# The expert loop of a hybrid decoder layer: down halves moved into the next pass, weight chunks of 1024 columns, SwiGLU on halves

## The reference, cut to what matters

```python
def moe(x2d, w_router, b_router, w_in, b_in, w_out, b_out):
    logits = (x2d @ w_router).astype(jnp.float32) + b_router.astype(jnp.float32)
    top_val, top_idx = lax.top_k(logits, TOP_K)
    gates = jax.nn.softmax(top_val, axis=-1)
    ...
    def expert_block(args):
        xb, e = args
        h = xb @ w_in[e] + b_in[e]
        glu = jnp.minimum(h[:, ::2], SWIGLU_LIMIT)
        lin = jnp.clip(h[:, 1::2], -SWIGLU_LIMIT, SWIGLU_LIMIT)
        act = glu * jax.nn.sigmoid(SWIGLU_ALPHA * glu) * (lin + 1.0)
        return act @ w_out[e] + b_out[e]
    ...
    y = y_buf[dest] * g_s[:, None].astype(y_buf.dtype)
    return jax.ops.segment_sum(y, tok_s, num_segments=N)
```

## Time and profile before

| what | value |
|---|---|
| median of 3 runs | 1720.86 us (1720.2 to 1728.64) |
| the profiled execution | 1725.17 us, of which the span of the trace is 1723.1 us |
| TensorE matmul busy | 1598.6 us (93%), 7671 instructions |
| TensorE weight load busy | 1259.6 us (73%) |
| VectorE busy | 1446.1 us (84%) |
| ScalarE busy | 1027.0 us (60%) |
| GpSimd busy | 153.7 us (9%) |
| DMA in a stretch of six passes | 95% of the 16 engines' time, 339 GB/s |
| mean granted TensorE clock | 0.956 of full |

### The profile page before, as it was taken

The page is one execution under the profiler, slowest core; times in us unless marked ns, Lnnn a source line. Parts: engine busy times, 40 slices in busy tenths (PEclk is TensorE's granted clock), DMA queues, the critical chain, the costliest instruction groups (busy, mean ns, idle before and its releaser), DMA issues.

```text
span 1723.1 us, 25611 instructions
## 1 busy us (share of the span) xinstructions
PE 1598.6 (93%) x7671; PEld 1259.6 (73%) x7671; DVE 1446.1 (84%) x1996; ACT 1027.0 (60%) x1067; POOL 153.7 (9%) x102
## 2 busy tenths in 40 slices
PE   3999688969999999999999999999999999999991
PEld 3999466737777777777777777777777777777771
DVE  4542742368999999999999999999999999999997
ACT  4221531226667666666776666676677666667673
POOL 0000311000010001000001000010000110001000
PEclk9999778959999999999999999999999999999996
DMA  7200701017999999999999999999999999999976
GB/s 249 98 26 1 245 0 43 25 37 272 344 331 351 339 338 338 346 341 336 346 333 347 343 337 349 336 343 334 335 350 334 340 347 341 336 344 347 337 271 249
DMA packets 243213, 476.46 MB, mean 277 GB/s; under 512 B 12784, under 2 KB 29808, under 8 KB 243120
## 3 DMA queue, kind: packets, MB, share of 16 engines
q1 hardware_dynamic: 229472, 445.23, 73.6%
q0 software_dynamic: 10128, 28.06, 4.4%
q10 hardware_dynamic: 3584, 2.78, 0.5%
HBM read 463.45 MB, written 21.50 MB: 281 GB/s over the span
## 4 chain that ended last, share of the span: by engine, by line
DVE 48%; issue 21%; ACT 3%; DVEq 3%; DMA 1%; SPq 0%
DVE split L1386 31%; DVE work L1402 3%; DVE work L1406 3%; ACT work L998 3%; DVE work L1399 3%; DVE operands L1392 1%; DVE work L1360 1%; DVE operands L1413 1%; DVEq L1347 1%; DMA ring<-expert_rows 1%; DVE operands L1381 1%; DVEq L124 0%; DVEq L1385 0%; DVE ring L1484 0%; DVE gate_next L1371 0%
## 5 line engine op out<-in xcount | busy, mean ns | idle before, releaser
L1386 DVE TENSOR_TENSOR split<-ring,split 128x2048 fp32r<-128x2048 f32 x398 | 892.5, 2283 | 4.0
L988 ACT CAST split<-ring 128x2048 fp32r<-128x2048 f32 x399 | 762.5, 1914 | 120.1 <-PE pair L789 113.0
L785 PE MATMUL pair<-split,operands 128*128 128x512 f32 x1584 | 650.4, 411 | 4.4 <-issue 4.4
L786 PE MATMUL pair<-split,operands 128*128 128x512 f32 x1584 | 628.4, 397 | 0.0
L789 PE MATMUL pair<-split,operands 128*128 128x512 f32 x1584 | 438.9, 399 | 7.9 <-DVE split L1386 7.9
L785 PEld LDWEIGHTS pair<-split,operands 128*128 128x128 f32 x1584 | 298.8, 189 | 98.0 <-issue 36.8
L789 PEld LDWEIGHTS pair<-split,operands 128*128 128x128 f32 x1584 | 293.4, 189 | 95.7 <-DVE split L1386 28.0
L786 PEld LDWEIGHTS pair<-split,operands 128*128 128x128 f32 x1584 | 298.8, 189 | 61.9
L998 ACT ACTIVATE work<-work 128x256 f32<-128x256 f32 x132 | 55.2, 418 | 251.8 <-DVE work L1399 251.8
L1546 POOL DMA_INDIRECT expert_rows<-work,dest_cur x33 | 84.0, 2545 | 665.8 <-ACT work L1011 625.2
L544 PE MATMUL pair<-split,operands 128*128 128x256 f32 x384 | 94.6, 284 | 8.6 <-issue 8.6
(11 more groups left out here) (205 smaller groups left out, 1299.3 us busy)
## 6 DMA issues: line engine op xcount, KB each, us to landing
ring<-in_w_moe_in SPq DMA_DIRECT2D x264, 1024.0 KB, 6.8
ring<-in_w_moe_out SPq DMA_DIRECT2D x132, 1024.0 KB, 6.8
ring<-in_w_in SPq DMA_DIRECT2D x12, 1024.0 KB, 10.9
ring<-expert_rows SPq DMA_DIRECT2D x3, 2048.0 KB, 10.1
late_ring<-in_w_o SPq DMA_DIRECT2D x4, 1024.0 KB, 9.6
resid<-in_x SPq DMA_DIRECT2D x4, 512.0 KB, 6.8
h_rows<-work ACTq DMA_DIRECT2D x4, 512.0 KB, 2.7
late_ring<-expert_rows SPq DMA_DIRECT2D x4, 512.0 KB, 9.0
```

Source lines behind the costliest of these rows:

```text
L785: pe.matmul(dst, left_hi[:, k0 + k, :], hi[s][:, k, :], start=(start and k == 0), stop=False)
L786: pe.matmul(dst, left_lo[:, k0 + k, :], hi[s][:, k, :], start=False, stop=False)
L988: act.copy(hi[j % PARTS], raw[j % RAW]).then_inc(hi_made, 1)
L1386: dve.tensor_tensor(lo[j % PARTS], raw[j % RAW], hi[j % PARTS].bitcast(F32), ALU.subtract).then_inc(lo_made, 1)
```

## The change

- **Order of the work.** The down products of pass p - 1 are moved into pass p, between the two halves of its up products. A pass is now: 4 chunks of the first up half of its expert, 4 down chunks of the expert before, 4 chunks of the second up half. The first pass has only the 8 up chunks, and four down chunks follow the last pass. The dummy chunks after the last pass are gone, and `parts` use the ring's slots in another order with other waits.
- **Chunks.** A chunk is now 256 rows of 1024 columns (still 1 MB; each row of it is 4 KB in a piece, where it was 2 KB). A product still has 12 matmuls of 512 columns, now two rows' blocks by two banks.
- **Bias.** `pick_bias` and `b_in_parts` span 128 partitions, the added ones zero, and the bias of a half is two matmuls of 128 rows. GpSimd adds 1 to the odd biases once.
- **SwiGLU.** Two halves of 512 results each: the sigmoid reads PSUM directly, and VectorE has three operations of 512 columns.
- **Token list.** `onehot` and `route_cur` are float32r, so that the list is four matmuls of that type; the gate's rest is the fourth column. VectorE builds the one-hot in one operation.
- **GpSimd.** It takes over `prepare_list` (three copies and a subtraction), `pick` (one copy) and the copies of destination and gate (`keep_lists`, three), eight small operations a pass which read SBUF. The scatter of pass p - 1 stands in pass p.
- **Transposes.** The activations' are two groups of four; the token rows' eight are two groups of four in different places, ahead of the last two up products.

```diff
-GW = 512
 KH = KT // 2
+HALF = 1024
+QUARTERS = KT // 2
 CHUNKS = 12
-IN_CHUNKS = 8
+DOWN, SECOND = 4, 8
 RAW = 6
 PARTS = 3
 SLOTS = P
 MAX_PASSES = SEQ * TOPK // SLOTS + NE - 1
-AHEAD = 3
-LO_AHEAD = 2
-STEPS_PER_PASS = 13
+STEPS_PER_PASS = 4
+STEPS_TO_ROUTE = 5
+ACT_LIMIT = LIMIT / (1.0 + math.exp(-SWI_ALPHA * LIMIT))
...
+raw = [ring[:, s].rearrange("p k c -> p (k c)").rearrange("p (k c) -> p k c", c=HALF) for s in range(RAW)]
...
+def up_chunk(e, half, k):
+    rows = of_expert(w_moe_in, e).rearrange("e (a k p) c -> a (e p) k c", p=P, a=QUARTERS)[k]
+    return rows[:, :, half * HALF:(half + 1) * HALF]
+def down_chunk(e, k):
+    return of_expert(w_moe_out, e).rearrange("e (a k p) c -> a (e p) k c", p=P, a=QUARTERS)[k]
+class Step:
+    def __init__(self, p, j):
+        first = isinstance(p, int) and p == 0 and j < DOWN
+        self.number = j if first else p * CHUNKS + (j - DOWN)
+        self.slot = j if first else (j + 2) % RAW
+        self.buffer = j % PARTS if first else (j + 2) % PARTS
+        self.fill = 1 if first else p * 2 + (j + 2) // RAW
...
+    def load(p, j, src):
+        c = Step(p, j)
+        sp.wait_ge(hi_made, c.number + (1 - RAW))
+        sp.wait_ge(lo_made, c.number + (1 - RAW))
+        sp.dma_start(raw[c.slot], src).then_inc(raw_full[c.slot], 16)
...
     def one_pass(p):
+        e, before = expert_of(p), expert_of(p - 1)
+        for k in range(QUARTERS):
+            load(p, k, up_chunk(e, 0, k))
+        for k in range(QUARTERS):
+            load(p, DOWN + k, down_chunk(before, k))
+        for k in range(QUARTERS):
+            load(p, SECOND + k, up_chunk(e, 1, k))
...
+    done = after_last(sp)
+    last = expert_of(done - 1)
+    for k in range(QUARTERS):
+        load(done, k, down_chunk(last, k))
...
+            sp.wait_ge(hi_made, all_used + (-4, -2, 0)[r])
+            sp.wait_ge(lo_made, all_used + (-4, -2, 0)[r])
...
     def product(p, j, dst, k0, left_hi, left_lo, start, stop):
+        pe.wait_ge(hi_made, c.number + 1)
+        for k in range(2):
+            for f in range(2):
+                cols = slice(f * 512, (f + 1) * 512)
+                pe.matmul(dst[:, f, :], left_hi[:, k0 + k, :], hi[c.buffer][:, k, cols],
+                          start=(start and k == 0), stop=False)
+                pe.matmul(dst[:, f, :], left_lo[:, k0 + k, :], hi[c.buffer][:, k, cols],
+                          start=False, stop=False)
+        pe.wait_ge(lo_made, c.number + 1)
+        for k in range(2):
+            for f in range(2):
+                cols = slice(f * 512, (f + 1) * 512)
+                mm = pe.matmul(dst[:, f, :], left_hi[:, k0 + k, :], lo[c.buffer][:, k, cols],
+                               start=False, stop=(stop and k == 1))
...
+    def bias_of_half(g):
+        for f in range(2):
+            at_f = (2 * g + f) * 512
+            pe.matmul(pair[g][:, f, :], pick_bias, b_in_parts[:, at_f:at_f + 512], start=True, stop=False)
+    def up(p, g, k):
+        product(p, g * SECOND + k, pair[g], 2 * k, xT_hi, xT_lo, False, k == QUARTERS - 1)
+    def down(p, j, k):
+        product(p, j, pair[2], 2 * k, actT_hi, actT_lo, k == 0, k == QUARTERS - 1)
...
+    def first_half(p, before):
+        pe.wait_ge(pick_ready, p + 1)
+        if before:
+            pe.wait_ge(half_read, p * 2 - 1)
+        bias_of_half(0)
+        pe.wait_ge(xT_lo_made, p * 2 + 1)
+        up(p, 0, 0)
+        up(p, 0, 1)
+        pe.wait_ge(xT_lo_made, p * 2 + 2)
+        up(p, 0, 2)
+        if before:
+            act_transposes(p - 1, 1)
+        up(p, 0, 3)
+    def second_half(p, before):
+        if before:
+            pe.wait_ge(half_read, p * 2)
+        bias_of_half(1)
+        up(p, 1, 0)
+        act_transposes(p, 0)
+        up(p, 1, 1)
+        pe.wait_ge(idx_ready, p + 2)
+        x_transposes(p + 1, 0)
+        up(p, 1, 2)
+        pe.wait_ge(actT_lo_made, p * 2 + 1)
+        x_transposes(p + 1, 1)
+        up(p, 1, 3)
...
     def one_pass(p):
+        first_half(p, True)
+        pe.wait_ge(down_banks_free, p)
+        pe.wait_ge(actT_lo_made, p * 2 - 1)
+        down(p, DOWN, 0)
+        token_list(p + 1)
+        down(p, DOWN + 1, 1)
+        pe.wait_ge(actT_lo_made, p * 2)
+        down(p, DOWN + 2, 2)
+        down(p, DOWN + 3, 3)
+        second_half(p, True)
...
+    done = after_last(pe)
+    pe.wait_ge(down_banks_free, done)
+    down(done, 0, 0)
+    act_transposes(done - 1, 1)
+    down(done, 1, 1)
+    pe.wait_ge(actT_lo_made, done * 2)
+    down(done, 2, 2)
+    down(done, 3, 3)
...
     def sigmoid(p, g):
+        last = Step(p, g * SECOND + QUARTERS - 1)
+        act.wait_ge(chunk_used, last.number + 1)
+        if not (isinstance(p, int) and p == 0 and g == 0):
+            act.wait_ge(act_ready, p * 2 + g)
+        glu = pair[g].rearrange("p b (c a) -> p a b c", a=2)[:, 0]
+        act.activation(sig.rearrange("p (b c) -> p b c", b=2), glu, ACT.Sigmoid, scale=SWI_ALPHA)\
+            .then_inc(sig_ready, 1)
...
+    def scale_rows(p, j):
+        act.wait_ge(chunk_used, Step(p, j).number + 1)
+        act.wait_ge(lists_kept, p + 1)
+        act.activation(y_rows.rearrange("p (f c) -> p f c", f=2), pair[2][:, :, :], ACT.Copy, scale=gate_cur[:, 0:1])\
+            .then_inc(down_banks_free, 1)
...
     def one_pass(p):
+        x_hi(p, 0)
+        make_hi(p, 0)
+        make_hi(p, 1)
+        x_hi(p, 1)
+        make_hi(p, 2)
+        sigmoid(p - 1, 1)
+        make_hi(p, 3)
+        make_hi(p, 4)
+        make_hi(p, 5)
+        act_hi(p - 1, 1)
+        make_hi(p, 6)
+        sigmoid(p, 0)
+        for j in range(7, 11):
+            make_hi(p, j)
+        scale_rows(p, DOWN + 3)
+        act_hi(p, 0)
+        make_hi(p, 11)
...
+    def slots_one_hot(p):
+        dve.wait_ge(route_ready, p + 1)
+        dve.tensor_tensor(onehot, slot_id.unsqueeze(1).to_broadcast([P, NT, SLOTS]),
+                          slot_from[:, :].unsqueeze(2).to_broadcast([P, NT, SLOTS]), ALU.is_equal)\
+            .then_inc(onehot_ready, 1)
...
+        wait(dve, lists_kept, p)
+        chain(dve.tensor_scalar(list_next[:, 0:1], bank[6][:, 0:1], NOWHERE, None, ALU.add))
+        chain(dve.tensor_reduce(list_next[:, 1:2], bank[6][:, 2:4], AX_X, ALU.add))
+        chain.settle()
+        dve.tensor_copy(token_next[:, :], bank[6][:, 1:2]).then_inc(idx_ready, 1)
...
     def swiglu(p, g):
+        glu, shifted = (pair[g].rearrange("p b (c a) -> p a b c", a=2)[:, a] for a in range(2))
+        gate, line, result = (m.rearrange("p (b c) -> p b c", b=2) for m in (sig, lin, act_rows[:, g, :]))
+        dve.wait_ge(sig_ready, p * 2 + (g + 1))
+        chain(dve.tensor_scalar(line, shifted, LIMIT + 1.0, 1.0 - LIMIT, ALU.min, ALU.max))
+        dve.scalar_tensor_tensor(gate, glu, LIMIT, gate, ALU.min, ALU.mult).then_inc(half_read, 1)
+        chain.settle()
+        dve.wait_ge(half_read, p * 2 + (g + 1))
+        dve.scalar_tensor_tensor(result, gate, ACT_LIMIT, line, ALU.min, ALU.mult).then_inc(act_ready, 1)
...
     def one_pass(p):
+        x_lo(p, 0)
+        make_lo(p, 0)
+        make_lo(p, 1)
+        x_lo(p, 1)
+        make_lo(p, 2)
+        swiglu(p - 1, 1)
+        make_lo(p, 3)
+        make_lo(p, 4)
+        slots_one_hot(p + 1)
+        make_lo(p, 5)
+        act_lo(p - 1, 1)
+        make_lo(p, 6)
+        swiglu(p, 0)
+        make_lo(p, 7)
+        read_list(p + 1)
+        for j in range(8, 11):
+            make_lo(p, j)
+        act_lo(p, 0)
+        make_lo(p, 11)
...
+    for still in (b_in_parts[2 * NE:P, :], pick_bias[2 * NE:P, :]):
+        dve.memset(still.bitcast(F32), 0.0).then_inc(b_in_split, 1)
...
+    def prepare_list(p, e):
+        if not (isinstance(p, int) and p == 0):
+            pool.wait_ge(list_ready, p)
+            pool.sem_inc(pool_passed, 1)
+        chain(pool.tensor_copy(first_cur[:, :], col(pass_first, p)))
+        chain(pool.tensor_copy(route_cur.unsqueeze(2), of(route, e)))
+        chain(pool.tensor_copy(pos_cur[:, :].unsqueeze(2), of(slot_of, e)))
+        chain.settle()
+        pool.sem_inc(pool_passed, 1)
+        pool.tensor_scalar(slot_from[:, :], pos_cur[:, :], first_cur[:, 0:1], None, ALU.subtract)\
+            .then_inc(route_ready, 1)
+    def pick(p, e):
+        if not (isinstance(p, int) and p == 0):
+            pool.wait_ge(chunk_used, Step(p - 1, SECOND).number + 1)
+            pool.sem_inc(pool_passed, 1)
+        pool.tensor_copy(pick_bias[0:2 * NE, :], col(expert_rows, e).to_broadcast([2 * NE, SLOTS]))\
+            .then_inc(pick_ready, 1)
...
+    def keep_lists(cur):
+        if cur:
+            chain(pool.tensor_copy(dest_cur[:, :], list_mid[:, 0:1]))
+            chain(pool.tensor_copy(gate_cur[:, :], list_mid[:, 1:2]))
+            chain.settle()
+            pool.sem_inc(pool_passed, 1)
+        pool.tensor_copy(list_mid[:, :], list_next[:, :]).then_inc(lists_kept, 1)
...
     def one_pass(p):
+        following = expert_of(p + 1)
+        prepare_list(p + 1, following)
         gather(p + 1)
-        scatter(p)
```

(61 more changed lines are left out.)

348 lines of the change are left out of this document (119 added, 229 removed).

## The result

The changed kernel takes 1740.96 us (median of 4 runs, 1739.97 to 1747.88) against 1723.76 us for the kernel before beside it: ratio 1.0106, 95% interval 1.0083 to 1.0129. It is 1% slower; 1640 us was predicted. The profiled execution took 1740.34 us, its span is 1738.5 us. One execution of a later kernel (the one whose sums wait, 1640.85 us) took 3866.52 us; it is left out of every ratio, and no run tells its cause.

What follows compares the result with a forecast made beforehand. VectorE was taken as full at 39.1 us a pass, TensorE hardly less. From 1723.1 us, 33 passes at 37.0 us give -73, start -3.7, pass 0 +3.8, end -8: 1642 us span, 1640 us median, range 1622 to 1705.

Steps and rivals of the forecast that it cites:

- TensorE's pass, 37.0 us: Loop pass on TensorE: products 33.7, bias 0.9, token list 0.45, transposes 1.9 us; 37.0 us for 39.24 before.
- the low end that was chosen: Bias on TensorE: 0.23 us per matmul of 128 rows, range 0.23 to 0.52; the high end costs 1.2 us a pass.
- VectorE's pass, 33.8 us: Loop pass on VectorE: its operations sum to 33.8 us, 5.3 us less than now, so VectorE stops being the bound.
- The gather: Next pass's token rows: landing at 28.2 us, wanted by TensorE at 30.0 us; 1.8 us of slack, the smallest found.
- The gather is late: Rival, chance 0.17: lo operations hold the gather; a second one makes TensorE wait 1.5 us in 32 passes, 1688 us.
- DMA doesn't set the pace: Rival, chance 0.08: if DMA's mean can't pass 350 GB/s, a pass takes 38.0 us, 1672 us in all.
- GpSimd's small operations: Rival, chance 0.10: lo holds the operations before the token list, the list is 4 to 5 us late, about 1800 us.
- Start: Kernel start: with the first x_lo ahead, the first product starts at about 386.9 us, worth -3.7 us.
- Pass 0's wait: First pass, without down products: its gather takes 10.3 us against 6.5 us of TensorE's work, +3.8 us.
- End: After the last product: without dummies the first three parts are summed earlier, sums near 1702, worth -8 us.
- The sum: Whole kernel: 1723.1 - 73 - 3.7 + 3.8 - 8 = 1642 us of span, 1640 us for the median.

## Why the prediction was wrong, point by point

- **TensorE's pass, 37.0 us:** right. At full clock it is busy 36.96 us; two bias matmuls take 1089.41 - 1088.95 = 0.46 us, the low end that was chosen. Without waits a pass takes 36.76 us.
- **VectorE's pass, 33.8 us:** 34.2 us, right.
- **The gather, "the rows land 6.3 us on the earlier trace rows, at 28.2 ... 1.8 us of slack":** this is the step that failed. The dates were right (start at 21.86 us, wanted at 29.95 us); the landing, taken from a gather among short operations, was 3.6 us too short. It comes at 31.8 us, 1.8 us late, and each us of wait costs a third more by the clock. The text had this outcome as a rival, *The gather is late*, and gave it 0.17 and 1688 us. Its evidence, a scatter of 2.60 us under lo, already spoke for a hold in the order that was forecast, and the forecast's own slack was smaller than one lo. But the rival had the way to it half wrong. It took one lo to hold the gather for 1.3 us and the rows to be still in time then, at 29.3 (28.2 + 1.3 is 29.5), and needed a second lo for its 31.5. The trace shows one lo, 1.1 us, and 2.5 us more between the instruction's end and the landing, for which the rival had no price, only "more if 4 KB packets of weights crowd it"; 2 KB packets gave 0.7 us of it. Its 1.5 us a pass were too small as well, for 1.95 of wait and, for the clock, nothing where 0.63 us a pass on average were lost (37.58 - 36.95).
- **The other rivals.** DMA doesn't set the pace of after: the kernels with the gather in time move 363 to 365 GB/s for 1,000 us. Their DMA share is 0.98 to 0.99, though, so little is left there. GpSimd's small operations are held, up to 2.32 us, 35 of the loop's 248 for over 2 us, but 0.6 us on average, and slot_from is ready at 1091.1, 9 us before VectorE's one-hot at 1100.18: not starved. The Trainium skill ("SBUF — State Buffer", section "Who interferes with whom") has such operations exclude each other, and the trace agrees: the copy that starts at 1088.17 under a lo lasts 2.04 us, to 1090.21. The same section reports that a tensor_tensor of VectorE, as lo is, was not seen to stall a DMA of GpSimd's; here gather and scatter do stall, their instruction ends 0.9 us after the end of the lo that it met, and the measurement decides.
- **Start:** the first product starts at 385.59, 1.3 us before the forecast. Pass 0's wait is 7.5 us, not 3.8.
- **End, "sums near 1702. That is worth -8 us":** mis-sized. It left out the loop's exit, 7.65 us, the half clock behind it, 1.9 us (the first product takes 4.8 us for 2.8), and the scatter held by the sums: from the last scale's start to the end 30.9 us, 4.6 more than the 26.3 that were forecast (1723.1 - 8 - 1688.8). With the scatter let through it is 24.2.
- **The sum:** 1642 + 33 x 2.53 (the pace, 39.53 for 37.0) + 3.7 (pass 0) + 14.1 (end) - 1.3 (start) = 1742 us of span, for 1738.5 measured.

What stays open is the part of the landing behind the instruction. From its end to the landing it is 5.1 us in before, 6.0 with lo kept away, 7.2 with read_list ahead of the SwiGLU, where no lo runs beside the instruction either, 7.6 in after and 8.0 with read_list 2.2 us earlier. So it is not a matter of the hold alone. The records of the gather's own 128 packets split it: the first packet starts 1.9 us behind the instruction's end in before, 2.4 with lo kept away and 3.1 in after, and from the first to the end of the last it is 2.8, 3.4 and 4.1 us, though a packet itself takes about 0.17 us in each. So the packets start later and further apart. Packet size is a part of the reason; the weight load issued ahead of the instruction's end (1.6 us behind the gather's start in after) may be another, and no run varied it alone.

Nor is it known which wait brings the lower clock. In after none of the eleven waits under 1.86 us was followed by it, all six over 2.30 us were, and of the fourteen between seven; the pass shown first, with 2.27 us of wait, kept its full clock, and so did one of 2.40 us with 2 KB packets.

## What to carry to other kernels

When a pipeline's margin is a few us, price the DMAs that GpSimd issues for the place that they will have, beside the VectorE operations that will then run, not by their median where they stand now; if the margin is smaller than one such operation, expect them late, start them earlier, or let VectorE wait until the instruction has run: 2.2 us of idle VectorE bought 2.9 us a pass here. A semaphore that the issuing queue raises behind a DMA instruction doesn't say that the instruction has run. Work that is moved behind a loop pays for the loop's exit; ask what the iterations that are skipped cost.

## What the hardware showed

- Sums of 1.14 us with both operands in SBUF, back to back, held GpSimd's scatter for 8.71 us, to 0.87 us after the last of them; three lo of 2.2 us, also back to back, let a gather through behind the first. With a wait for a semaphore put ahead of the sixth sum, which cost VectorE 0.05 us in all, the sums too let the scatter through behind one: 1.97 us.
- A stand of TensorE of about 2 us was followed by half the granted clock for some 3.6 us in 13 of after's 31 passes: 1.86 us of wait then cost 3.4 us.
- A semaphore raised by GpSimd's queue behind an indirect DMA let VectorE's next operation start 0.09 us ahead of the DMA's instruction; a memset of 0.13 us that GpSimd executes behind it started as the instruction ended (993.70 and 993.72).
- Fourteen skipped iterations of loop and test cost TensorE 7.65 us, 0.55 us each.
